# Output projection by token tiles inside the attention block of a decoder layer: ten of 32 products in the block's last run, no block boundary before the rest

## The reference

```
proj = rmsnorm(x, mix_norm) @ w_in            # q, k, v of both groups of 8 heads
o_sb = stick_breaking_attention(q_sb, k_sb, v_sb)
o_dl = dilated_mixture_attention(rotary(q_dl), rotary(k_dl), v_dl)
merged = concat(rmsnorm(o_sb, sb_out_norm), rmsnorm(o_dl, dil_out_norm))
x = x + merged @ w_out
```

## Time and profile before

| | us |
|---|---|
| median of 3 runs (range) | 2082.76 (2081.71 to 2083.47) |
| the profiled execution | 2083.61 |
| its span, first to last instruction | 2081.8 |
| TensorE busy | 1932.0 (93%) |
| VectorE, ScalarE, POOL busy | 1257.5, 908.3, 753.1 |
| mean granted TensorE clock | 0.964 |
| last run of the heads' block, from the scores of its step 1 | 1238.20 to 1297.85 |
| products of the output block | 1308.52 to 1404.8 |

### The profile page before, as it was taken

One profiled execution on the slowest core, in us unless ns is written; L12 is line 12 of the kernel. 1 busy time (PEld: TensorE's weight loads), 2 busy tenths in 40 slices (PEclk: granted clock), 3 DMA queues, 4 the chain that ended last, 5 costly groups with the idle time before them and its releaser, 6 DMA issues. The chain is left out here.

```text
span 2081.8 us, 25977 instructions
## 1 busy us (share of the span) xinstructions
PE 1932.0 (93%) x9224; PEld 1582.6 (76%) x9224; DVE 1257.5 (60%) x1649; ACT 908.3 (44%) x1467; POOL 753.1 (36%) x506
## 2 busy tenths in 40 slices
PE   5899999999999898989989976896999999999998
PEld 4788888888888676767767755685788888888886
DVE  6855556555556266676676677327856556554555
ACT  6433333333335455555555555306433333333334
POOL 2656656530000252242242335304656556540000
PEclk9999999999999999999999986897999999999999
DMA  3443544558664310010101112511534435458663
GB/s 143 153 166 131 193 151 144 190 192 290 195 192 144 116 46 26 21 56 25 51 25 40 31 36 70 193 41 71 186 143 160 174 132 185 152 203 308 192 192 142
DMA packets 95584, 276.01 MB, mean 133 GB/s; under 512 B 10480, under 2 KB 14704, under 8 KB 89840
## 3 DMA queue, kind: packets, MB, share of 16 engines
q1 hardware_dynamic: 95472, 274.59, 38.7%
HBM read 190.14 MB, written 80.22 MB: 130 GB/s over the span
## 5 line engine op out<-in xcount | busy, mean ns | idle before, releaser
L703 PE MATMUL banks<-ffn_x_operands_hi 128*128 128x512 f32 x616 | 239.8, 389 | 0.0
L706 PE MATMUL banks<-ffn_x_operands_hi,ffn_x_operands_lo 128*128 128x512 f32 x616 | 239.7, 389 | 0.0
L705 PE MATMUL banks<-ffn_x_operands_lo,ffn_x_operands_hi 128*128 128x512 f32 x616 | 239.6, 389 | 0.0
L1265 DVE TENSOR_TENSOR heads_wt<-banks,heads_wt 128x512 fp32r<-128x512 f32 (+1 forms) x160 | 100.9, 632 | 134.7 <-ACT heads_wt L1109 133.9
L1382 PE MATMUL banks<-first_hi,w_hi 128*128 128x512 f32 x384 | 161.1, 420 | 13.5 <-ACT heads_qk_raw L1131 7.9
L401 ACT ACTIVATE scaled_rows<-banks 128x512 f32<-128x512 f32 x132 | 78.6, 595 | 201.9 <-PE banks L690 201.9
L516 DVE TENSOR_TENSOR scaled_rows<-banks,scaled_rows 128x512 f32<-128x512 f32 x132 | 91.1, 690 | 118.1 <-PE banks L690 74.4
L986 POOL TENSOR_TENSOR scaled_rows<-scaled_rows,heads_stay 128x128 f32<-128x128 f32 (+7 forms) x64 | 86.1, 1351 | 210.9 <-DVE heads_stay L1225 210.9
L1384 PE MATMUL banks<-first_hi,w_lo 128*128 128x512 f32 x384 | 152.2, 396 | 0.0
L1383 PE MATMUL banks<-first_lo,w_hi 128*128 128x512 f32 x384 | 152.0, 396 | 0.0
L687 PE MATMUL banks<-first_hi,ffn_w_ring_hi 128*128 128x512 f32 x352 | 139.1, 395 | 11.8 <-DVE first_lo L567 11.8
(11 more groups left out here) (183 smaller groups left out, 4821.0 us busy)
## 6 DMA issues: line engine op xcount, KB each, us to landing
w_raw<-in_ffn_w_gate SPq DMA_DIRECT2D x22, 1024.0 KB, 6.8
ffn_up_raw<-in_ffn_w_up SPq DMA_DIRECT2D x22, 1024.0 KB, 6.1
ffn_down_raw<-in_ffn_w_down SPq DMA_DIRECT2D x22, 1024.0 KB, 4.9
down_operands<-ffn_down_raw SPq DMA_DIRECT2D x22, 1024.0 KB, 7.3
w_raw<-h_operands SPq DMA_DIRECT2D x52, 256.0 KB, 3.0
ffn_up_raw<-h_operands SPq DMA_DIRECT2D x52, 256.0 KB, 3.0
ffn_down_raw<-h_operands SPq DMA_DIRECT2D x50, 256.0 KB, 3.0
w_raw<-in_w_in SPq DMA_DIRECT2D x24, 512.0 KB, 4.0
```

Of the source, the lines that this page charges most:

```text
L703: pe.matmul(out, hi[:, 0, tok], hi[:, 1, :], start=(opens and c == 0), stop=False, skip_group_check=True)
L705: pe.matmul(out, hi[:, 0, tok], lo[:, 1, :], start=False, stop=False, skip_group_check=True)
L706: last = pe.matmul(out, lo[:, 0, tok], hi[:, 1, :], start=False, stop=(c == NP - 1), skip_group_check=True)
L1265: dve.tensor_tensor(wt[:, wt_slot(s, j), 0:tiles, 1, :], b.ps[:, bank, 0:tiles * P].rearrange("p (t c) -> p t c", c=P), wt[:, wt_slot(s, j ...
```

## The change

The output block is gone. Its work is in the heads' block:

- Products 0 to 9 stand behind the values of banks 10 to 19 of the last run, one behind each. All ten write PSUM bank 7, and product m waits until product m-1 has been added. VectorE adds product m-1 behind the low part of the next bank (`behind_slot`). Products 10 to 31 follow; 10 and 11 stand between the last values, and from 10 on the banks are m % 3.
- The result is taken in eight token tiles of 128 tokens instead of four quarters. ScalarE makes the high part and the squares of tiles 0 to 5 behind banks 3, 4, 6, 8, 14 and 18 of the last run, and of tiles 6 and 7 behind it. POOL now makes the low part, and folds the squares.
- A result tile comes in two parts: seven of its eight feature tiles from DRAM, the last one, which the last run itself makes, straight from `o_stage` by two transfers for each tile. The last run stores nothing to DRAM.
- The output weights are loaded ahead of the last run's first steps, in four transfers of two feature tiles, most of them into the memory of `x`, which now lies over tiles that are used only before the last run. ScalarE makes two high parts behind each of steps 0 to 3; POOL keeps the even low parts, VectorE makes the odd ones behind steps 1 to 4.
- Sums of squares: tiles 0 to 2 behind bank 9 into bank 7 of PSUM (so product 0 waits for their root), tiles 3 and 4 behind bank 18, the others behind products 15 and 19.
- SP's order in the last run is new: weights, `x`, the store of the run before, tiles, and the stores of `x` between them.

The core of the diff. `last_run` comes first as SP's list and then as POOL's, `result_tile` first as POOL's and then as ScalarE's part; `behind_slot` is VectorE's, called behind the low part of bank n with `slot` n - 1, and the rest is TensorE's.

```diff
+OUT_TILES = 4
+OUT_SUMS = ((0, 1, 2), (3, 4), (5, 6), (7,))
+SUMS_IN_SLOT = {9: 0, 18: 1}
+SUMS_BEHIND = {15: 2, 19: 3}
+FIRST_SLOT = 10
+IN_SLOTS = BANKS - FIRST_SLOT
+TILE_IN_SLOT = {3: 0, 4: 1, 6: 2, 8: 3, 14: 4, 18: 5}
...
+        BANK_OUT, BANK_SUM = 7, 3
+        def out_bank(m):
+            return BANK_OUT if m < IN_SLOTS else m % 3
...
+            def last_run():
+                sp.wait_ge(w_split, 2 + 6 * PAIRS)
+                load_out_weights(0)
+                sp.wait_ge(sb_weights, 2 * STEPS * PAIRS)
+                sp.wait_ge(rot_split, 1 + ROTATED * PAIRS)
+                for i in range(1, KT // 2):
+                    load_out_weights(i)
+                load_x(0)
+                store_part(PAIRS - 1, SB_KIND, 1)
+                sp.wait_ge(pv_ready, 4 + BANKS * run(PAIRS - 1, DIL_KIND))
+                for part in range(2):
+                    sp.wait_ge(o_stored[part], 32 * 2 * PAIRS)
+                load_o(0)
+                load_o(1)
+                last_features(0)
+                last_features(1)
+                for t in range(2, 4):
+                    load_o(t)
+                    last_features(t)
+                load_o(4)
+                sp.wait_ge(out_w_split, KT)
+                for pair in range(1, TT // 2):
+                    load_x(pair)
...
+            def result_tile(t):
+                pool.wait_ge(o_hi_done, t + 1)
+                pool.tensor_tensor(o_lo[t % OUT_TILES][:, :, :], o_raw[t % 2][:, :, :],
+                                   o_hi[t % OUT_TILES][:, :, :].bitcast(F32), ALU.subtract).then_inc(o_split, 1)
+                pool.wait_ge(o_squared, t + 1)
+                pool.tensor_tensor(o_sq[:, :, 0:2, :], o_sq[:, :, 0:2, :], o_sq[:, :, 2:4, :], ALU.add
+                                   ).then_inc(o_halved, 1)
+                pool.wait_ge(o_halved, t + 1)
+                if t >= OUT_TILES:
+                    pool.wait_ge(sums_ready, 1 if t < 7 else 2)
+                pool.tensor_tensor(o_fold[:, t % OUT_TILES, :, :], o_sq[:, :, 0, :], o_sq[:, :, 1, :], ALU.add
+                                   ).then_inc(o_folded, 1)
+            def last_run():
+                split_out_weights(0)
+                split_out_weights(2)
+                result_tile(0)
+                split_out_weights(4)
+                result_tile(1)
+                split_out_weights(6)
+                for t in range(2, TT):
+                    result_tile(t)
...
+            def result_tile(t):
+                act.wait_ge(o_loaded[t % 2], 48 * (t // 2 + 1))
+                if t >= OUT_TILES:
+                    act.wait_ge(y_ready, 4 * (t - OUT_TILES + 1))
+                act.activation(o_hi[t % OUT_TILES][:, :, :], o_raw[t % 2][:, :, :], ACT.Copy).then_inc(o_hi_done, 1)
+                if t > 0:
+                    act.wait_ge(o_folded, t)
+                act.activation(o_sq[:, :, :, :].rearrange("p g f c -> p (g f) c"), o_raw[t % 2][:, :, :], ACT.Square
+                               ).then_inc(o_squared, 1)
...
+            def behind_slot(slot):                 
+                if slot in SUMS_IN_SLOT:
+                    reciprocals(SUMS_IN_SLOT[slot])
+                if slot >= FIRST_SLOT:
+                    add_product(slot - FIRST_SLOT)
...
+            def out_product(m):
+                t, half, group = m // 4, m % 4 // 2, m % 2
...
+                if m == 0:
+                    pe.wait_ge(out_w_split, KT)
+                    pe.wait_ge(root_done, 1)
+                elif m < IN_SLOTS:
+                    pe.wait_ge(y_added, m)
+                if m == IN_SLOTS:
+                    pe.wait_ge(dil_max, 2 * STEPS * PAIRS)
+                if m >= IN_SLOTS + 3:
+                    pe.wait_ge(y_added, m - 2)
+                pe.wait_ge(o_split, t + 1)
...
+            def in_slot(slot):
+                if slot in SUMS_IN_SLOT:
+                    sums(SUMS_IN_SLOT[slot])
+                if slot >= FIRST_SLOT:
+                    out_product(slot - FIRST_SLOT)
...
-def output_block(nc, b, sem, w_split_buffers, o_split_buffers, o_dram, x_dram):
```

More of the change, by code:

```diff
@@ L866, in heads_block @@
         o_stored = [sem(f"o_stored{h}") for h in range(2)]
+        o_loaded = [sem(f"out_o_loaded{i}") for i in range(2)]
+        x_loaded = [sem(f"out_x_loaded{t}") for t in range(TT // 2)]
+        o_hi_done, o_split, o_squared = sem("out_o_hi_done"), sem("out_o_split"), sem("out_o_squared")
+        o_halved, o_folded, x_stored = sem("out_o_halved"), sem("out_o_folded"), sem("out_x_stored")
+        ones_set, sums_ready, root_done, rstd_done = (sem(f"out_{n}") for n in ("ones", "sums", "root", "rstd"))
+        y_ready, y_added = sem("out_y_ready"), sem("out_y_added")
         block = ctx.enter_context(nc.Block())
@@ L973, in _ @@
             one_run(PAIRS - 1, SB_KIND, more=False)
-            one_run(PAIRS - 1, DIL_KIND, project=False, more=False)
-            for h in range(2):
-                sp.wait_ge(o_stored[h], 32 * (2 * PAIRS + 1))
+            last_run()
+            b.x_stored = x_stored
         @block.gpsimd
@@ L1011, in projected_lo, with step @@
                                    qk_hi[SB_KIND][piece][:, cols].bitcast(F32), ALU.subtract).then_inc(sb_split, 1)
-            def step(it, kind, s, project=True, last=False):
+            def step(it, kind, s):
                 it1, kind1 = pair_of(it, kind, 1)
@@ L1017, in step @@
                         products(it, s + 1)
-                elif not last and kind1 == SB_KIND:
+                elif kind1 == SB_KIND:
                     products(it1, 0)
-                if project and ENDS.get(s, HALVES) < ROTATED:
+                if ENDS.get(s, HALVES) < ROTATED:
                     if kind1 == DIL_KIND:
@@ L1175, in step @@
                         elementwise(nit, nkind, ns, 1)
+                    if last and slot_of(s, j) in TILE_IN_SLOT:
+                        result_tile(TILE_IN_SLOT[slot_of(s, j)])
+                    if last and slot_of(s, j) in SUMS_IN_SLOT:
+                        roots(SUMS_IN_SLOT[slot_of(s, j)])
                 if project and kind1 == DIL_KIND and ENDS.get(s - 1, HALVES) < ROTATED:
@@ L1186, in step @@
                     split_weights(*pair_of(it, kind, 2), Q)
-                if last:
-                    split_out_weights(s)
+                if last and 2 * s < KT:
+                    split_out_weights(2 * s)
+                    split_out_weights(2 * s + 1)
                 if last and s == STEPS - 1:
                     values_low(it, kind, s)
+                    result_tile(6)
+                    result_tile(7)
+                    for i in sorted(SUMS_BEHIND.values()):
+                        roots(i)
             def one_run(it, kind, first=0, end=STEPS, project=True, last=False):
@@ L1330, in step @@
                         rotate(*rot)
+                    if last:
+                        behind_slot(slot_of(s, j) - 1)
                 if ahead and nkind == DIL_KIND:
@@ L1477, in step @@
                     values_behind(it, kind, s, j, 2)
+                    if last:
+                        in_slot(slot_of(s, j))
                 if proj:
@@ L1480, in step, with sums @@
                 if last and s == STEPS - 1:
+                    out_product(IN_SLOTS)
                     values_behind(it, kind, s, banks_of(s) - 1, 1)
+                    out_product(IN_SLOTS + 1)
                     values_behind(it, kind, s, banks_of(s) - 1, 0)
+                    for m in range(IN_SLOTS + 2, PRODUCTS_OUT):
+                        out_product(m)
+                        if m in SUMS_BEHIND:
+                            sums(SUMS_BEHIND[m])
+            def sums(i):
+                if i == 0:
+                    pe.wait_ge(ones_set, 1)
+                if i == 1:
+                    pe.wait_ge(dil_max, 2 * STEPS * PAIRS)
+                if i > 1:
+                    pe.wait_ge(root_done, i)
+                pe.wait_ge(o_folded, OUT_SUMS[i][-1] + 1)
+                for n, t in enumerate(OUT_SUMS[i]):
+                    for group in range(2):
+                        c = 2 * n + group
+                        last = pe.matmul(b.ps[:, sums_bank(i), c:c + 1], o_fold[:, t % OUT_TILES, group, :], unit[:, :],
+                                         start=(c == 0), stop=True, skip_group_check=True)
+                last.then_inc(sums_ready, 1)
```

333 lines of the change are left out of this document (135 added, 198 removed).

## The result

| | before | after |
|---|---|---|
| median of 4 runs each, us | 2082.36 | 2095.39 |
| range, us | 2081.71 to 2083.47 | 2094.16 to 2095.76 |
| ratio, 95% interval | | 1.0061 (1.0044 to 1.0078) |
| the profiled execution, us | 2083.61 | 2095.76 |

The change makes the kernel 13.0 us slower. I had forecast 2089.0, slower, in a range that reaches to 2105. The forecast's own narrower range, 2085 to 2094, was missed by 1.4 us.

What follows compares the result with a forecast made beforehand. The last run is a ring PE, ACT, DVE, PE with no engine full; TensorE fills the output block. Stretch A +17.3, Stretch B +30.7, Stretch C -44.8 and clock +3 sum to +6.2: 2089.0 us, range 2075 to 2105.

Steps and rivals of the forecast that it cites:

- the ring: Banks 11 to 19: product, transposes, high part, low part, addition form a closed chain on one PSUM bank, 5.6 us a bank.
- Stretch C: Behind bank 19, to the last addition: 22 products at 2.72 us without the standstill, 106.9 to 62.1 us, gain 44.8.
- Stretch B: Banks 11 to 19 of the last run: nine products not hidden, 23.8 to 54.5 us, 30.7 more.
- The clock: Lower clock in the last run's new banks: 3 us taken, about one fall of a bank, bounds 0 and 26.
- Rival (2): Clock falls in the last run's stalls, half the ten banks at half clock: 14.5 us instead of 3, 2100; chance 0.15.
- Stretch A: Last run up to bank 11's turn: tiles, weights, root and product 0 make it 17.3 us later, bounds 6 and 24.
- the wait for tile 3's transfers: Ahead of bank 9: ScalarE waits 3 us for tile 3's load, counted as part of the delay.
- the estimate that I hung on it: Up to bank 11: VectorE's four low parts of weights also wait for POOL, 5 us longer; not in the sum.
- the first of the two scalings in steps 3 and 4: VectorE's scaling ahead of bank 9, newly beside POOL's work: 2.18 us instead of 0.55.
- (1): Faster: the ten banks ahead of product 0 hide the tiles in ScalarE's waiting, Stretch A below 11 us, 2078; chance 0.24.
- (3): POOL becomes the bound ahead of product 0, which comes 5 us later: +11, 2094; chance 0.11.
- (4): The ten products in the run exactly eat what barrier and standstill give: 0, 2083; chance 0.10.

Runs made afterwards that it cites:

- after again: The changed kernel, unchanged, run and profiled a second time against the kernel before: 2094.57 us, ratio 1.0059.
- no table: The changed kernel with the root taken by a square instead of a square root, so no table is loaded (values wrong): 2091.68 us, ratio 1.0048.
- the addition first: The changed kernel with VectorE adding product m-1 ahead of the next bank's low part instead of behind it: 2070.51 us, ratio 0.9947.
- the narrow ones: On top of the addition first, VectorE's four low parts of weights cover 64 of 1024 columns (result wrong): 2067.74 us, ratio 0.9938.
- before again: The kernel before, unchanged, run and profiled a second time: 2084.24 us, ratio 1.0010 to its other runs.

## Why the prediction was right, and which term was off

The direction, the ring in B and the gain in C were right. The size was not: the sum gave +6.2 us, the marks of the profiles +9.7 and the medians +13.0. The first gap is explained below; the second is not (see Open).

**Stretch C: right.** 44.3 us gained where the steps said 44.8: twenty-two products at 2.72 and no gap ahead of products 20 or 24. The last addition (last line of VectorE's fence below) is as in the earlier trace rows, with 1.97 us of idle time and 0.75 of work.

**Stretch B: the ring right, bank by bank.** From turn to turn, the extra of a half clock product (over 2.90) taken off:

| bank | measured | less clock | forecast |
|---|---|---|---|
| 11 | 7.4 | 5.8 without the scores | 5.6 |
| 12 | 8.7 | 8.9 with the scores (1.6) | 8.8 |
| 13 | 8.1 | 6.6 | 6.4 |
| 14, 15, 16 | 5.6, 4.9, 5.6 | the same | 5.6, 4.9, 5.6 |
| 17 | 7.9 | 6.4 | 6.4 |
| 18 | 5.6 | the same | 5.6 |
| 19 | 7.4 | 5.8 | 5.6 |
| sum | 61.1 | 55.2 | 54.5 |

The 8.8 for bank 12 isn't the sum of the terms that I gave: 5.6, 1.6 for the scores and one masked maximum make 8.5, with both 9.9. That it met 8.9 is partly luck.

That the additions close the ring is shown, not only argued: turning two calls around in VectorE's queue took TensorE's 17.3 us of waiting to 0.5. My sentence "because one PSUM bank serves them all" named half of the cause, though; with the queue in the other order one bank is enough.

**The clock: the term that was mis-sized.** I took 3 us. Products 2, 3, 7 and 9 lasted 4.28, 4.44, 4.40 and 4.45 instead of 2.90: 6.0 us. I had leaned on the feed-forward's window at 1.00 with 2.43 of 5 us busy; the row did not carry over to products with 2 to 3 us of standstill between them. Rival (2) had the mechanism right and put its price at 14.5, more than twice what it cost. B has 0.89 in all three profiles with the ring (after, after again, no table), and 1.00 in all five with the addition first, which is why undoing the ring returned more than the ring's waits. Each fall cost about 1.5 us, half of the 2.9 that the rival's sum took. The 3.5 us between +6.2 and +9.7 are B's 3.4, of which the clock is 3.0, with C's 0.5 and A's -0.4.

**Stretch A: the sum right, three steps wrong, so in part by luck.** Product 0 started 50.6 us into the run; 1286.5 less 1235.82 had been 50.7. Bank 9's high part came 9.65 late, 10.3 forecast. But the wait for tile 3's transfers, which I had put in the chain, was beside it: moving the tile changed nothing. What stood in the chain was VectorE, whose queue made the draining of step 3 late. Its timeline in after, with three of the four low parts of weights (L1504) and a scaling (L1402), and then POOL's:

```profile
1250.92 1.28 DVE L1504 SCALAR_TENSOR_TENSOR first_lo<-w_raw,gains_sb,first_hi 128x1024 fp32r<-128x1024 f32 x1
...
1268.55 2.46 DVE L1402 TENSOR_SCALAR scaled_rows<-scaled_rows,heads_row_inv 128x640 f32<-128x640 f32 x1
1270.94 2.29 DVE L1504 SCALAR_TENSOR_TENSOR first_lo<-x_second,gains_sb,first_hi 128x1024 fp32r<-128x1024 f32 x1
...
1282.30 1.75 DVE L1504 SCALAR_TENSOR_TENSOR first_lo<-x_second,gains_sb,first_hi 128x1024 fp32r<-128x1024 f32 x1
...
1416.69 0.75 DVE L1522 SCALAR_TENSOR_TENSOR x_second<-banks,heads_rstd,x_second 128x512 f32<-128x512 f32 x1 [1.97 <-PE banks L1720]
```

```profile
1251.39 2.56 POOL L1141 TENSOR_TENSOR x_second<-x_second,gains_sb 128x1024 f32<-128x1024 f32 x1 [1.13 <-ACT first_hi L1267]
...
1268.06 2.61 POOL L1149 TENSOR_TENSOR heads_o_lo<-heads_o_raw,heads_o_hi 128x1024 fp32r<-128x1024 f32 x1
1270.63 1.51 POOL L1152 TENSOR_TENSOR heads_o_sq<-heads_o_sq 128x512 f32<-128x512 f32 x1
1272.22 1.59 POOL L1157 TENSOR_TENSOR heads_o_fold<-heads_o_sq 128x256 f32<-128x256 f32 x1
1273.77 1.89 POOL L1141 TENSOR_TENSOR x_second<-x_second,gains_sb 128x1024 f32<-128x1024 f32 x1
```

A low part of the weights takes VectorE 1.28 us undisturbed (1250.92), 2.29 from 1270.94 and 1.75 from 1282.30 beside POOL; and where VectorE was first, POOL's multiply took 2.56 (1251.39) instead of 1.89 (1273.77). The trace agrees with the Trainium skill, "SBUF — State Buffer", section "Who interferes with whom", that a VectorE instruction with two SBUF inputs and a GpSimd instruction that reads SBUF exclude each other, and that the one that issues first goes on. But the estimate that I hung on it, 5 us, was too high: of the four low parts only two met POOL while behind it, for 1.0 + 0.5 us, and the narrow ones met it at the same two places.

The other two steps: I had counted the first of the two scalings in steps 3 and 4 as slow beside POOL, like the second. It wasn't: the two over 640 keys took 0.68 and 2.46 us, in before 0.55 and 2.18. And product 0 did not wait for the root, as my sum had it, but for TensorE's own sums, 2.41 us at half clock for which A had no term; the two limits lie 0.5 us apart in after and change places in its second profile. So waits that I hadn't counted stand in the sum in place of those for tile 3 and the tables. How much each of them is worth, the runs don't say more closely than this.

By the runs, A's 16.9 us are some 5.9 for the tiles, 3.7 for the early weights and low parts, 1.3 for the root's sums and 6.0 for product 0 and the half clock just ahead of it. Each is a difference between two profiles, good to about 1 us, since the clock rises at other places in each (bank 11 came at 55.14 in after and at 54.55 in its second profile).

**The rivals.** (1), faster because ScalarE's old idle time takes in the tiles, fell: A was 16.9, not under 11. (3), POOL as the bound, fell: POOL was busy 37.60 of 55.14 us and its last fold ahead of product 0 ended at 1282.97, 1.8 us before the sums that needed it, which TensorE reached without a gap. (4), nothing gained or lost, was near in B and C (37.1 against 44.3) and fell by A.

**Open.** The profiled executions are 12.15 us apart: 9.74 in the three stretches, 0.3 behind them, and 2.1 before the run begins, where the code is the same. I put the last down to where the clock rises and falls upstream, which is not shown: a window of 682 to 690 has 0.71 before and 0.61 after, but in the second pair 0.61 before and 0.69 after, and the runs' starts of all twelve profiles scatter from 1235.2 to 1239.0, with the second pair 0.7 apart. The medians of the first pair differ by 13.0, its marks by 9.7. For after again the medians are 12.3 apart, or 10.3 if before again alone is taken, whose marks are 10.6 apart. Whether 2 us or so are a steady cost upstream, no run here tells.

## What to carry to other kernels

Filling an engine's idle time with new work only pays if the new work's own chain doesn't run through the wait that made the idle time: ask in whose queue the release of the new buffer stands, and behind what. Here a finished product lay behind an instruction that waited for the next bank, and moving one call was worth 25 us, almost twice what the change had cost. Count the clock as part of such a wait: where the standstills go, half clock may go with them.

## What I had not expected of the hardware

Dense matmuls with standstills of 0.9 to 3.3 us between them did not hold the clock: B has 0.89 in two profiles of the same kernel, with falls in products 2, 3, 7 and 9 both times, while a window of the feed-forward kept 1.00 at a smaller busy share. And the moment at which the clock rises decides over single products: product 0, first after a long stretch of small matmuls, lasted 4.55 us in one profile of after, 4.30 in the other, and 2.77 in a kernel that differs by the root's function alone. It even decides what product 0 waits for, TensorE's own sums or the root on ScalarE. A difference of 1.3 us that equals a table load (1.28) was the clock.
